# First pair, last pair and end of a hybrid encoder step: banks, order and token halves

## The chip, the cores and the metric

The kernel runs on one core of a Trainium2 chip. The metric is the device time of one execution in microseconds (us). TensorE (PE, with its weight loads PEld), VectorE (DVE), ScalarE (ACT), GpSimd (POOL) and SyncE (SP) run streams of their own and hand work on by semaphores.

## What is computed

One layer for 512 prompt tokens and 32 sample tokens (TOK = 544), with D = 1024, 8 heads of 64, and weights in fp32:

```python
xn = rms_norm(x, g_mix)
u, q, k, v, gates = split(xn @ w_in)                # 512 | 512 | 512 | 512 | 2048 columns
gate_a, gate_b = split(sigmoid(gates + b_gate))
y_pool = (trailing_mean(u) - u) @ w_pool_grp * scale # 4 groups, windows 2, 4, 8, 16
y_sb = stick_breaking(q, k, v)                       # a = exp(log_sigmoid(z) + later log_sigmoid(-z)), causal
x = x + (gate_a * (y_pool @ w_pool_up) + gate_b * (y_sb @ w_sb_up)) @ w_out
x = x + square(relu(rms_norm(x, g_mlp) @ w_up)) @ w_down
x = x + sigmoid(rms_norm(x, g_ple) @ w_ple_gate) * (p @ w_ple_proj)
y = rms_norm(x, g_final)
```

k, v and the pooling state are outputs too.

## The kernel before

Features lie on partitions, tokens on columns. A result of 128 features x 544 tokens takes two PSUM banks of 272 columns, a "slot" (banks 2s and 2s+1). Products in fp32 precision are made of three passes over high and low parts: hi*hi, hi*lo, lo*hi. Each weight tile (512 KB) is loaded by SP into `raw`, its high part is made by ScalarE (`split`, L691, later `hi`, L699), its low part by VectorE (`split`, L1448, later `ahead`, L1456), in a ring of four (`AHEAD` = 3 tiles ahead). SP loads tile t when the low part of tile t-2 is made.

The order of the work is written out by hand in each engine's block. Stage 1 has four pairs of heads, `pair(i)`, each with eight tiles: q, k, v, u, then four gate tiles; pair 0 and pair 3 are written out, 1 and 2 are a loop. TensorE's tile is 48 matmuls. A head's attention goes: `scores` (z into banks 4 to 6), `chain` on ScalarE (Abs, Exp, Ln), `stick` on VectorE (L1532), masks on GpSimd (L634), `stick_later`, `stick_hi` and `stick_lo` (sums over keys, high and low parts), `sums` on TensorE (L1114), `prob` on ScalarE (L778), masks, `prob_hi` and `prob_lo` (L1553), `outputs` on TensorE (L1140). The second head's `sums` and `outputs` run within the next pair. `v_rows` transposes v into bank 7. VectorE multiplies each result by the inverse norm `rn`, which scales tokens, since the norm is taken beside the products: `square` (L715) and `add_square` (L1473) sum the squares, `first_stats` sums over partitions by a matmul with -1 (L1091), `variance` (L1481), `root` (Ln, Exp), `root_step` (L1486 to L1488).

In pair 0 results 0, 1, 2 lie in slots 0, 1, 2 and result 3 (u) in slot 0 again (`result_slot`). TensorE's order there: tiles 0, 1, 2 with the norm's sums (into banks 6 and 7) behind step 1 of tile 2, tile 3, `scores(0)`, `v_rows`, tiles 4 and 5, `sums(0)`, tile 6, `outputs(0)`, `scores(1)`, tile 7.

In pair 3 the four group maps of the pooling (`group`, L1042) need the high and low parts of the means (`mean_hi`, `mean_lo` L1573); those of groups 2 and 3 are made after ScalarE's `chain(1)` and VectorE's `stick(1)`.

The last stage makes the gate of the embedding in two groups of seven products (`product_of`, L1352, SIDES A11, S1, S2, S4, S3, A12, A22; a Strassen-like scheme in which each result is a quarter: half of the group's features x half of the tokens). The second group is followed by four `embedding` tiles (L1042 to L1044), `embedded` (L1881 multiply, L1883 add to x), ScalarE's squares (L1021), five sums over partitions (`stat3`, L1430), Ln and Exp (L1028, L1031), L1481 to L1488, then the final scaling of eight tiles of 128 x 544: six by VectorE (L1916), two by GpSimd (L676), each stored by SP (L570).

## Time and profile before

| | us |
|---|---|
| median of 3 runs | 793.26 (792.95 to 793.46) |
| the profiled execution | 793.77 |
| its span | 791.9 |
| PE busy | 773.7 (98%) |
| DVE busy | 494.8 (62%) |
| ACT busy | 381.5 (48%) |
| POOL busy | 96.9 (12%) |

The span is the time from the first to the last event that the profiler saw on the core. TensorE's busy time is modelled at its end (a matmul is pipelined), so the starts of its matmuls are to be read, and the idle time in brackets behind a row.

### The profile page before, as it was taken

To read this page: it belongs to the slowest core of one execution; us is meant where nothing else is said; L and a number is where in the kernel's file an instruction comes from. 1 tells how busy PE (TensorE), PEld (TensorE's weight loads), DVE (VectorE), ACT (ScalarE), POOL (GpSimd) and SP (SyncE) were. 2 spreads that over 40 slices of the span, in tenths; PEclk is the share of its full clock that TensorE was granted. 3 is DMA by queue.
4 is the path that set the end of the run, shared out by engine and by line. 5 is a ranking of instruction groups with operands and counts; after the bars stand their busy time and mean duration, and the time that the engine had idled before them with its cause. 6 is when DMAs were issued, how large, how long until landed. Compare 5 with 4: busy or idle time off the path is not lost.

```text
span 791.9 us, 14329 instructions
## 1 busy us (share of the span) xinstructions
PE 773.7 (98%) x6050; PEld 765.2 (97%) x6050; DVE 494.8 (62%) x606; ACT 381.5 (48%) x443; POOL 96.9 (12%) x169
## 2 busy tenths in 40 slices
PE   8899999999999999999999999999999999999993
PEld 8899999999999899999999999999999999999993
DVE  5876566566566547787763367434763367677965
ACT  6554534535575443665641255213642155555643
POOL 1040140150150000020001100020001100100001
PEclk9999999999999999999999999999999999999998
DMA  7342231232221316786566847587575856826402
GB/s 236 99 125 74 70 120 53 82 105 56 98 90 55 107 54 206 240 202 178 179 171 168 202 160 206 139 188 183 158 192 145 204 171 180 195 82 161 119 1 113
DMA packets 33097, 110.18 MB, mean 139 GB/s; under 512 B 4496, under 2 KB 4496, under 8 KB 33040
## 3 DMA queue, kind: packets, MB, share of 16 engines
q1 hardware_dynamic: 24768, 84.72, 32.4%
q0 software_dynamic: 6016, 21.04, 14.9%
q10 hardware_dynamic: 2256, 3.60, 1.3%
q8 instruction: 44, 0.72, 0.4%
q14 instruction: 13, 0.11, 0.0%
HBM read 94.33 MB, written 4.52 MB: 125 GB/s over the span
## 4 chain that ended last, share of the span: by engine, by line
PE 90%; DVE 5%; ACT 2%; issue 1%; DMA 1%; SPq 1%; DVEq 0%; ACTq 0%
PE psum L1352 24%; PE psum L1061 19%; PE psum L1067 19%; PE psum L1064 19%; PE psum L1114 1%; DMA xt<-x_t 1%; PE psum L1042 1%; PE psum L1142 1%; PE psum L1043 1%; PE psum L1044 1%; PE psum L1140 1%; PE psum L1430 1%; PE psum L1102 1%; DVE work L1473 1%; PE psum L1101 1%
## 5 line engine op out<-in xcount | busy, mean ns | idle before, releaser
L699 ACT ACTIVATE w_hi<-raw_more 128x1024 fp32r<-128x1024 f32 x84 | 88.7, 1056 | 133.0 <-PE psum L1067 100.7
L1064 PE MATMUL psum<-b_lo,w_hi 128*128 128x272 f32 x688 | 142.0, 288 | 0.0
L1061 PE MATMUL psum<-b_hi,w_hi 128*128 128x272 f32 x672 | 139.3, 288 | 0.0
L1067 PE MATMUL psum<-b_hi,w_lo 128*128 128x272 f32 x672 | 138.8, 288 | 0.0
L1061 PE MATMUL psum<-a_hi,w_hi 128*128 128x272 f32 x576 | 120.8, 291 | 3.3 <-DVE a_lo L1462 1.2
L1456 DVE TENSOR_TENSOR w_lo<-raw_more,w_hi 128x1024 fp32r<-128x1024 f32 x84 | 102.2, 1222 | 34.6 <-ACT w_hi L699 34.3
L1067 PE MATMUL psum<-a_hi,w_lo 128*128 128x272 f32 x576 | 119.0, 288 | 0.0
L1064 PE MATMUL psum<-a_lo,w_hi 128*128 128x272 f32 x576 | 118.8, 288 | 0.0
L1352 PE MATMUL psum<-u_hi,w_hi 128*128 128x272 f32 x560 | 115.9, 288 | 0.2 <-ACT h_of L933 0.2
L1352 PE MATMUL psum<-u_hi,w_lo 128*128 128x272 f32 x560 | 115.7, 288 | 0.0
L1352 PE MATMUL psum<-u_lo,w_hi 128*128 128x272 f32 x560 | 115.5, 287 | 0.0
L1064 PEld LDWEIGHTS psum<-b_lo,w_hi 128*128 128x128 f32 x688 | 108.1, 188 | 0.0
L1061 PEld LDWEIGHTS psum<-b_hi,w_hi 128*128 128x128 f32 x672 | 105.4, 188 | 0.8 <-issue 0.7
L1067 PEld LDWEIGHTS psum<-b_hi,w_lo 128*128 128x128 f32 x672 | 105.1, 189 | 0.0
L1061 PEld LDWEIGHTS psum<-a_hi,w_hi 128*128 128x128 f32 x576 | 90.2, 188 | 4.4 <-DVE a_lo L1462 2.0
L1064 PEld LDWEIGHTS psum<-a_lo,w_hi 128*128 128x128 f32 x576 | 90.5, 189 | 0.0
L1067 PEld LDWEIGHTS psum<-a_hi,w_lo 128*128 128x128 f32 x576 | 90.0, 189 | 0.0
L1352 PEld LDWEIGHTS psum<-u_hi,w_hi 128*128 128x128 f32 x560 | 87.9, 188 | 0.5 <-issue 0.4
L1352 PEld LDWEIGHTS psum<-u_lo,w_hi 128*128 128x128 f32 x560 | 88.3, 188 | 0.0
L1352 PEld LDWEIGHTS psum<-u_hi,w_lo 128*128 128x128 f32 x560 | 87.5, 188 | 0.0
L1742 DVE TENSOR_TENSOR xt<-psum,xt 128x544 f32<-128x544 f32 x40 | 28.9, 723 | 88.2 <-PE psum L1067 88.2
L1448 DVE TENSOR_TENSOR w_lo<-raw,w_hi 128x1024 fp32r<-128x1024 f32 x41 | 51.8, 1265 | 41.5 <-ACT w_hi L691 41.3
(245 smaller groups left out, 1010.3 us busy)
## 6 DMA issues: line engine op xcount, KB each, us to landing
raw_more<-w_tiles SPq DMA_DIRECT2D x84, 512.0 KB, 4.3
raw<-w_tiles SPq DMA_DIRECT2D x66, 512.0 KB, 3.5
raw_more<-w_tiles POOLq DMA_DIRECT2D x16, 512.0 KB, 6.7
raw_more<-raw_more POOLq DMA_DIRECT2D x14, 512.0 KB, 8.3
xt<-x_t SPq DMA_DIRECT2D x8, 272.0 KB, 6.2
y_t<-xt SPq DMA_DIRECT2D x8, 272.0 KB, 2.5
raw<-w_tiles POOLq DMA_DIRECT2D x4, 512.0 KB, 7.6
raw_more<-raw POOLq DMA_DIRECT2D x3, 512.0 KB, 6.4
```

The costliest lines, as they stand in the source:

```text
L699: act.activation(w_hi[:, t % W_RING, :, :].rearrange("p k c -> p (k c)"), src, ACT.Copy)\
L1042: pe.matmul(out, hi, rhi, start=first, stop=False, skip_group_check=True)
L1043: pe.matmul(out, hi, rlo, start=False, stop=False, skip_group_check=True)
L1044: return pe.matmul(out, lo, rhi, start=False, stop=last, skip_group_check=True)
L1061: pe.matmul(base[:, h, :], w_hi[:, s, wk, :], at(hi, k, h * HALF, (h + 1) * HALF), start=(opens and q == 0), stop=False, skip_group_check= ...
L1064: pe.matmul(base[:, h, :], w_hi[:, s, wk, :], at(lo, k, h * HALF, (h + 1) * HALF), start=False, stop=False, skip_group_check=True)
L1067: mm = pe.matmul(base[:, h, :], w_lo[:, s, wk, :], at(hi, k, h * HALF, (h + 1) * HALF), start=False, stop=(closes and q == len(ks) - 1), s ...
L1101: pe.matmul(z, b_lo[:, keys], b_hi[:, both], start=(b != 3), stop=False, skip_group_check=True)
L1352: mm = pe.matmul(out[:, two, :], w_part[:, t % W_RING, 2 * k + two, :], u_part[:, op, k, :], start=(OPENS[s] and k == 0 and w_part is w_hi ...
L1448: dve.tensor_tensor(w_lo[:, s, :, :].rearrange("p k c -> p (k c)"), raw[:, t % RAW_RING, :], w_hi[:, s, :, :].rearrange("p k c -> p (k c)" ...
L1456: dve.tensor_tensor(w_lo[:, t % W_RING, :, :].rearrange("p k c -> p (k c)"), src, w_hi[:, t % W_RING, :, :].rearrange("p k c -> p (k c)"), ...
L1742: dve.tensor_tensor(halves(xt[:, m, :]), slot(n), halves(xt[:, m, :]), ALU.add).then_inc(taken, 1)
```

## The change

- `result_slot`: result 3 (the first u) gets slot 3 (banks 6 and 7).
- The first norm's sums go into the free columns of banks 0 to 3 in four pieces, behind step 3 of tile 2 instead of step 1.
- Pair 0: tiles 3 and 4 come ahead of the first scores, then `v_rows`, tiles 5 and 6, `sums(0)`, tile 7, `outputs(0)`, `scores(1)`. The other engines' orders follow: ScalarE splits tiles 5, 6 and 7 ahead of `chain(0)`, VectorE splits 6 and 7 and reads the first gate ahead of `stick(0)`, and reads v's low half and splits tile 8 ahead of `stick_lo(0)`.
- Pair 3: the means of groups 2 and 3 are split ahead of `chain(1)` and `stick(1)`.
- The last group is followed by halves of tokens: five products, the second token half's two embeddings, A12, the first embedding of the first token half, the second half's norm sum, A22, the last embedding, the first half's sum. Sigmoids, squares, roots, scaling and stores go by quarters and halves; 16 stores of 136 KB stand for 8 of 272 KB. ScalarE loads the sigmoid table and the logarithm table once more.

```diff
@@ -100,10 +100,21 @@
         seq.extend((("down", c, q), q % 4, False) for q in range(KT))
     group("ple", 0, 0, "stat2")
     seq.extend((("proj", q), (2 + q) % 4, False) for q in range(KT // 2))
-    group("ple", 1, 1)
-    seq.extend((("proj", KT // 2 + q), q, False) for q in range(KT // 2))
-    seq.append((("stat3",), 0, False))
+    for what in LAST_ORDER:
+        if what[0] == "ple":
+            seq.append((what, 2 + (not IN_X[what[2]]), BY_ACT[what[2]]))
+        else:
+            seq.append((what, {"pj": what[-1], "stat3": 3 * what[-1]}[what[0]], False))
     return seq
+LAST_ORDER = ([("ple", 1, s) for s in range(5)] + [("pj", 1, 0), ("pj", 1, 1), ("ple", 1, 5), ("pj", 0, 0),
+              ("stat3", 1), ("ple", 1, 6), ("pj", 0, 1), ("stat3", 0)])
+PLE_PLACE = ((0, 1, 2, 3, 4, 5, 6, 7), (0, 1, 2, 3, 4, 6, 7, 5))
...
@@ -175,7 +187,7 @@
 def result_slot(n):
-    return (n if n < 3 else 0) if n < 4 else (n - N_ATT + 2) % 4 if n >= N_ATT else n % 2
+    return n if n < 4 else (n - N_ATT + 2) % 4 if n >= N_ATT else n % 2
...
@@ -385,7 +398,21 @@
             return h[:, half, :, :].rearrange("p n t -> p (n t)")
-        rn_ps = psum[:, 2:4, 0:HALF]
+        first_sums = psum[:, 0:4, HALF:HALF + HALF // 2]
...
@@ -558,17 +588,16 @@
...
-            sp.wait_ge(out_done, 16 * KT)
+            for nth, i in enumerate((1, 0)):
+                for k in range(KT):
+                    if k % 4 == 3:
+                        m = POOL_LAST[k // 4]
+                        sp.wait_ge(fin_pool, len(POOL_LAST) * nth + k // 4 + 1)
+                    else:
+                        m = BY_DVE[k - k // 4]
+                        sp.wait_ge(fin_done, len(BY_DVE) * nth + k - k // 4 + 1)
+                    sp.dma_start(y_t[m, :, tokens(i)], xt[:, m, tokens(i)]).then_inc(out_done, 16)
+            sp.wait_ge(out_done, 16 * 2 * KT)
...
@@ -669,11 +698,13 @@
...
+            for nth, i in enumerate((1, 0)):
+                pool.wait_ge(rn_done, nth + 1)
+                pool.wait_ge(fin_done, len(BY_DVE) * nth + 1)
+                for m in POOL_LAST:
+                    x = xt[:, m, tokens(i)]
+                    pool.tensor_tensor(x, x, rn[:, tokens(i)], ALU.mult).then_inc(fin_pool, 1)
...
@@ -814,18 +849,32 @@
...
                 act.dma_start(k_t[i, :, :], ev[:, 1, 0:TOK]).then_inc(kv_out[0], 16)
-                if not first:
-                    prob(1, i - 1)
+                if first:
+                    split(AHEAD + 2)
+                    act.wait_ge(taken, 3)
+                    act.dma_start(v_t[i, :, :], ev[:, 2, 0:TOK]).then_inc(kv_out[1], 16)
+                    split(AHEAD + 3)
+                    split(AHEAD + 4)
+                    chain(0, i)
+                    values_hi(i)
+                    split(AHEAD + 5)
+                    stick_hi(0, i)
+                    split(AHEAD + 6)
+                    prob(0, i)
+                    split(AHEAD + 7)
+                    prob_hi(0, i)
+                    chain(1, i)
...
@@ -842,10 +891,11 @@
                 if last:
                     group_hi(0)
                     group_hi(1)
-                chain(1, i)
-                if last:
+                    act.wait_ge(z_done, HEADS)
                     mean_hi(2)
                     mean_hi(3)
+                chain(1, i)
                 split(AHEAD + 7, i, S1_PER, 7)
                 if last:
...
+                act.wait_ge(res_done, KT // 2 + LAST_QUARTERS.index((half, i)) + 1)
+                act.activation(made(UP_GROUPS + 1, half, i), last_x(half, i), ACT.Square).then_inc(sq_done, 1)
+            def half_root(nth, i):
+                n = NTH[("stat3", i)]
+                r = ev[:, 1, tokens(i)]
+                act.wait_ge(full, n + 1)
+                act.activation(r, slot(n)[:, 0, :], ACT.Ln, scale=-1.0 / D_MODEL, bias=eps[:, 0:1]).then_inc(log_done, 1)
+                act.wait_ge(log_done, nth)
+                act.activation(r, r, ACT.Exp, scale=-0.5).then_inc(root_done, 1)
...
+            quarter_sigmoid(0, 1)
...
+            quarter_sigmoid(1, 1)
+            quarter_square(0, 1)
+            quarter_square(1, 1)
+            quarter_sigmoid(0, 0)
+            tables(LOG_EXP)
+            half_root(4, 1)
+            quarter_square(0, 0)
+            tables(SIGMOID)
+            quarter_sigmoid(1, 0)
+            tables(LOG_EXP)
+            quarter_square(1, 0)
+            half_root(5, 0)
+            act.wait_ge(rn_done, 2)
+            act.activation(rn_ps, rn[:, tokens(0)], ACT.Copy).then_inc(rn_copied, 1)
...
@@ -1176,10 +1245,13 @@
             def first_stats(q):
-                if q == 1:
+                if q == 3:
                     pe.wait_ge(const_made, N_CONST)
                     pe.wait_ge(sq_added, KT)
-                    stats(None).then_inc(stat0, 1)
+                    for b in range(4):
+                        mm = pe.matmul(first_sums[:, b, :], negone[:, :].bitcast(F32),
+                                       acc[:, b * HALF // 2:(b + 1) * HALF // 2], start=True, stop=True)
+                    mm.then_inc(stat0, 1)
...
@@ -1193,20 +1265,25 @@
                     weights(2)
                     dense(result(2), 2, ALL, A, aside=first_stats).then_inc(full, 1)
                     tile(3, i)
-                else:
-                    tile(0, i)
-                    tile(1, i)
-                    sums(1, i - 1)
-                    tile(2, i)
-                if first:
-                    pe.wait_ge(var_done, 1)
-                    pe.wait_ge(taken, 3)
-                else:
-                    outputs(1, i - 1)
+                    tile(4, i)
+                    pe.wait_ge(taken, 4)
+                    scores(0, i)
+                    v_rows(i)
+                    tile(5, i)
+                    tile(6, i)
+                    sums(0, i)
+                    tile(7, i)
+                    outputs(0, i)
+                    scores(1, i)
+                    return
+                tile(0, i)
+                tile(1, i)
...
+            def last_embedding(i, half):
+                t, n = t_ple(1, T_UP), NTH[("pj", i, half)]
+                weights(t)
+                place_for(n)
+                for k in range(PLE // P):
+                    c = slice(k * TOK + i * HALF, k * TOK + (i + 1) * HALF)
+                    for w_part, b_part in ((w_hi, b_hi), (w_hi, b_lo), (w_lo, b_hi)):
+                        for two in range(2):
+                            wk = k * (KT // 2) + 2 * half + two
+                            mm = pe.matmul(slot(n)[:, two, :], w_part[:, t % W_RING, wk, :], b_part[:, c],
+                                           start=(k == 0 and w_part is w_hi and b_part is b_hi),
+                                           stop=(k == PLE // P - 1 and w_part is w_lo), skip_group_check=True)
...
+            def last_sums(i):
+                n = NTH[("stat3", i)]
+                place_for(n)
+                pe.wait_ge(sq_added, 3 * KT + KT // 2 + i)
+                squares = [(acc[:, tokens(i)], 0)]
+                for half in range(2 - 2 * i):
+                    q = made(UP_GROUPS + 1, half, i)
+                    squares += [(q[:, two, :], KT // 2 + LAST_QUARTERS.index((half, i)) + 1) for two in range(2)]
+                for k, (of, nth) in enumerate(squares):
+                    if nth:
+                        pe.wait_ge(sq_done, 3 * KT + nth)
+                    mm = pe.matmul(slot(n)[:, 0, :], negone[:, :].bitcast(F32), of, start=(k == 0),
+                                   stop=(k == len(squares) - 1), skip_group_check=True)
+                mm.then_inc(full, 1)
...
+            for what in LAST_ORDER:
+                if what[0] == "ple":
+                    product_of(t_ple(1, what[2]), NTH[what], what[2]).then_inc(full, 1)
+                elif what[0] == "pj":
+                    last_embedding(what[1], what[2])
...
+                    last_sums(what[1])
...
@@ -1628,21 +1739,29 @@
...
-                                  rn[:, SEQ:TOK], ALU.mult).then_inc(taken, 1)
+                pool_input(i)
                 if first:
+                    split(AHEAD + 3)
+                    split(AHEAD + 4)
+                    gate(0, i)
                     stick(0, i)
-                    split(AHEAD + 3)
                     stick_later(0, i)
+                    values_lo(i)
+                    split(AHEAD + 5)
+                    stick_lo(0, i)
+                    gate(1, i)
+                    split(AHEAD + 6)
+                    gate(2, i)
+                    split(AHEAD + 7)
+                    prob_lo(0, i)
+                    gate(3, i)
+                    head_out(0, i)
+                    stick(1, i)
+                    stick_later(1, i)
+                    stick_lo(1, i)
...
@@ -1661,13 +1780,13 @@
                 head_out(0, i)
                 if last:
                     group_lo(1)
+                    mean_lo(2)
+                    mean_lo(3)
                 else:
                     split(AHEAD + 7, i, S1_PER)
                 stick(1, i)
                 if last:
-                    mean_lo(2)
                     gate(3, i)
...
+            def scaled_quarter(side):
+                n, i = NTH[("ple", 1, SIDES.index(side))], 1 if side == "S4" else 0
+                c = made(UP_GROUPS + 1, 0, i)
+                dve.wait_ge(taken, taken_count(n))
+                dve.tensor_tensor(c, c, rn_of[i], ALU.mult).then_inc(rel_done, 1)
+            def gated_quarter(half, i):
+                nth, n = LAST_QUARTERS.index((half, i)), NTH[("pj", i, half)]
+                h = made(UP_GROUPS + 1, half, i)
+                dve.wait_ge(psig_done, 2 + nth + 1)
+                dve.wait_ge(full, n + 1)
+                dve.tensor_tensor(h, slot(n), h, ALU.mult).then_inc(taken, 1)
+                dve.wait_ge(taken, taken_count(n))
+                dve.tensor_tensor(last_x(half, i), last_x(half, i), h, ALU.add).then_inc(res_done, 1)
...
+            def half_rms(nth, i):
...
+                dve.wait_ge(root_done, nth)
+                link(dve.scalar_tensor_tensor(out=t, in0=r, scalar=-0.5, in1=r, op0=ALU.mult, op1=ALU.mult))
+                dve.wait_ge(taken, taken_count(n))
+                link(dve.tensor_tensor(t, t, var[:, tokens(i)], ALU.mult))
+                dve.scalar_tensor_tensor(out=rn[:, tokens(i)], in0=t, scalar=1.5, in1=r, op0=ALU.add, op1=ALU.mult)\
+                   .then_inc(rn_done, 1)
...
+                ahead(T_PLE + T_UP + 1 + s)
+                if s < KT // 2:
+                    add_square(s, 3 * KT)
+                if SIDES[s] in ("S4", "S3"):
+                    add_quarter(UP_GROUPS + 1, NTH[("ple", 1, s)], s)
+                if SIDES[s] == "S4":
+                    scaled_quarter("S4")
+                if SIDES[s] == "S3":
+                    scaled_second(UP_GROUPS + 1, "S3")
+            gated_quarter(0, 1)
+            gated_quarter(1, 1)
+            dve.wait_ge(sq_done, 3 * KT + KT // 2 + 2)
+            two, other = made(UP_GROUPS + 1, 0, 1), made(UP_GROUPS + 1, 1, 1)
+            link(dve.tensor_tensor(two, two, other, ALU.add))
+            link(dve.tensor_tensor(acc[:, tokens(1)], acc[:, tokens(1)], two[:, 0, :], ALU.add))
+            dve.tensor_tensor(acc[:, tokens(1)], acc[:, tokens(1)], two[:, 1, :], ALU.add).then_inc(sq_added, 1)
+            add_quarter(UP_GROUPS + 1, NTH[("ple", 1, 5)], 5)
+            scaled_quarter("A12")
+            gated_quarter(0, 0)
+            half_rms(4, 1)
+            scaled_second(UP_GROUPS + 1, "A22")
+            dve.wait_ge(rn_done, 1)
+            for m in BY_DVE[:2]:
+                finished(m, 1, rn[:, tokens(1)])
+            gated_quarter(1, 0)
+            dve.wait_ge(res_done, KT // 2 + 4)
+            for m in BY_DVE[2:]:
+                finished(m, 1, rn[:, tokens(1)])
+            half_rms(5, 0)
+            dve.wait_ge(rn_done, 2)
+            for m in BY_DVE:
+                if m == BY_DVE[0]:
+                    finished(m, 0, rn[:, tokens(0)])
+                else:
+                    dve.wait_ge(rn_copied, 1)
+                    finished(m, 0, rn_ps)
```

## Rows read from the trace of the kernel before

**Rows 1.** Waits of TensorE over the span: waiter, releaser, us in total, times, longest.
```profile
PE psum L1061 <- DVE ev L1591: 1.2, 1, 1.2
PE psum L1042 <- DVE b_lo L1574: 0.6, 2, 0.3
```
**Rows 2.** Timeline, TensorE, pair 0: start us, us, engine, line, operation, [idle before <-releaser].
```profile
23.16 1.16 PE L1091 MATMUL psum<-work,negone 128*128 128x272 f32 x4 [0.35 <-DVE work L1473]
...
36.06 0.39 PE L1101 MATMUL psum<-b_hi,b_lo 128*128 128x512 f32 x1
...
37.27 0.62 PE L1152 MATMUL psum<-ident,ev 128*128 128x128 f32 x4
38.70 0.49 PE L1061 MATMUL psum<-a_hi,w_hi 128*128 128x272 f32 x2 [0.80 <-DVE upad L1636]
```
**Rows 3.** Timeline, VectorE, pair 0.
```profile
24.69 0.72 DVE L1481 TENSOR_SCALAR work<-psum 128x544 f32<-128x544 f32 x1
...
33.71 1.23 DVE L1448 TENSOR_TENSOR w_lo<-raw,w_hi 128x1024 fp32r<-128x1024 f32 x1
...
36.48 1.23 DVE L1448 TENSOR_TENSOR w_lo<-raw,w_hi 128x1024 fp32r<-128x1024 f32 x1
...
41.35 1.49 DVE L1532 SCALAR_TENSOR_TENSOR work<-psum,work 128x1280 f32<-128x1280 f32 x1 [2.80 <-ACT work L765]
...
48.83 0.55 DVE L1549 TENSOR_TENSOR later_lo<-later,later_hi 128x384 fp32r<-128x384 f32 x1
```
**Rows 4.** The page's DMA issues: count, KB each, us to landing.
```profile
raw<-w_tiles SPq DMA_DIRECT2D x66, 512.0 KB, 3.5
```
**Rows 5.** Timeline, GpSimd: the masks behind the stick steps of the first two heads.
```profile
42.91 1.96 POOL L634 TENSOR_SCALAR_AFFINE_SELECT work<-work 128x128 f32<-128x128 f32 x4 [38.85 <-DVE work L1532]
...
69.44 1.03 POOL L634 TENSOR_SCALAR_AFFINE_SELECT work<-work 128x128 f32<-128x128 f32 x4 [9.48 <-DVE work L1532]
```
**Rows 6.** Timelines around the start of pair 1, VectorE, ScalarE, TensorE.
```profile
67.88 1.48 DVE L1532 SCALAR_TENSOR_TENSOR work<-psum,work 128x1280 f32<-128x1280 f32 x1
...
80.00 0.72 DVE L1497 TENSOR_TENSOR ev<-psum,rn 128x544 f32<-128x544 f32 x1 [0.20 <-PE psum L1067]
...
86.04 1.49 DVE L1553 TENSOR_TENSOR b_lo<-work,b_hi 128x1280 fp32r<-128x1280 f32 x1
...
82.36 1.24 ACT L778 ACTIVATE work<-psum 128x1280 f32<-128x1280 f32 x1 [0.31 <-PE psum L1114]
...
79.80 0.40 PE L1114 MATMUL psum<-b_hi,negtri 128*128 128x512 f32 x1
...
88.22 0.40 PE L1140 MATMUL psum<-b_hi 128*128 128x512 f32 x1
```
**Rows 7.** Timeline, TensorE: the start of pool part 0 behind the group maps.
```profile
247.71 0.49 PE L1061 MATMUL psum<-mean_hi,w_hi 128*128 128x272 f32 x2 [0.34 <-issue]
```
**Rows 8.** The chain of waits (start us, us, what) and TensorE's timeline, last group.
```profile
748.28 21.01 PE psum L1352 x168
...
776.10 3.83 PE L1430 MATMUL psum<-h_two,negone 128*128 128x272 f32 x16
```
**Rows 9.** Timelines, ScalarE and VectorE: a table load, a 544-wide and a 272-wide step.
```profile
771.23 1.28 ACT L725 ACT_TABLE_LOAD   x1
...
782.92 0.72 DVE L1488 SCALAR_TENSOR_TENSOR rn<-ev 128x544 f32<-128x544 f32 x1
...
37.70 0.43 DVE L1633 TENSOR_TENSOR upad<-psum,rn 128x272 f32<-128x272 f32 x1
```
**Rows 10.** The view of the tile y_t: issue durations in ns, first and last start; landing.
```profile
L570 SPq DMA_DIRECT2D y_t<-xt x8: 332/400/652, 784.5 to 788.3; - x8
...
DMA to landing us min/median/max: 2.1/2.5/3.1
```
**Rows 11.** Stretches of the end: busy us of each engine, granted clock, DMA share, GB/s.
```profile
785.00:785.50 0.50, 0.00 (x0) 0.00 (x0) 0.50 (x2) 0.00 (x0) 0.50 (x1) 0.58 0.29 113
...
790.00:791.00 1.00, 0.00 (x0) 0.00 (x0) 0.00 (x0) 0.00 (x0) 0.00 (x0) 0.50 0.95 370
```

More of the change, by code:

```diff
@@ L134, in staged_loads @@
     seq.append(("proj", 0))
-    seq.extend((UP_GROUPS + 1, what) for what in LOADS)
+    seq.extend((UP_GROUPS + 1, what) for what in LOADS[:5])
     seq.append(("proj", 1))
+    seq.extend((UP_GROUPS + 1, what) for what in LOADS[5:])
     return seq
@@ L385, in made_half, with tokens, last_x @@
             return h[:, half, :, :].rearrange("p n t -> p (n t)")
-        rn_ps = psum[:, 2:4, 0:HALF]
+        first_sums = psum[:, 0:4, HALF:HALF + HALF // 2]
+        rn_ps = psum[:, 2, 0:HALF]
+        def tokens(i):
+            return slice(i * HALF, (i + 1) * HALF)
+        def last_x(half, i):
+            return xt[:, 4 * half + 2:4 * half + 4, tokens(i)]
+        LAST_QUARTERS = ((0, 1), (1, 1), (0, 0), (1, 0))
+        BY_DVE = [m for m in range(KT) if m not in POOL_LAST]
         rn_twice = rn[:, :].unsqueeze(1).broadcast_to([P, 2, TOK])
@@ L1017, in _ @@
-            tables(LOG_EXP)
-            for q in range(KT // 2, KT):
-                m = PROJ_ORDER[q]
-                act.wait_ge(res_done, q + 1)
-                act.activation(h_two[:, m // 4, m % 2, :], xt[:, m, :], ACT.Square).then_inc(sq_done, 1)
+            for s in range(T_UP):
+                n = NTH[("ple", 0, s)]
+                ahead(t_ple(0, s))
+                if s == 0:
+                    act.wait_ge(ulo_done, 3 * KT)
+                if s == 3:
+                    act.wait_ge(taken, taken_count(NTH[("stat2",)]))
+                    root(3)
+                    embedding_hi(0)
+                    embedding_hi(1)
+                if s == 5:
+                    tables(SIGMOID)
+                if s == T_UP - 1:
+                    gate_sigmoid(0, 0)
+                if BY_ACT[s]:
+                    copy_quarter(UP_GROUPS, n, s)
@@ L1085, in tile @@
                 dense(pair_result(j, i), j % W_RING, ALL, A).then_inc(full, 1)
-            def stats(n):
-                out = psum[:, 6:8, 0:HALF] if n is None else result(n)
-                for h in range(2):
-                    mm = pe.matmul(out[:, h, :], negone[:, :].bitcast(F32), acc[:, h * HALF:(h + 1) * HALF],
-                                   start=True, stop=True)
-                return mm
             def scores(hh, i):
@@ L1432, in _ @@
-            mm.then_inc(full, 1)
+            def last_embedding(i, half):
[11 more added lines that the diff above has]
+                mm.then_inc(full, 1)
@@ L1434, in _ @@
+            group_of("ple", 0, t_ple(0, 0), 3 * KT // 2, "stat2", 3 * KT)
+            for q in range(KT // 2):
+                embedding(q)
+            for what in LAST_ORDER:
[3 more added lines that the diff above has]
+                    last_embedding(what[1], what[2])
+                else:
+                    last_sums(what[1])
         @block.vector
@@ L1908, in _ @@
[L1908 to L1918 removed]
+            for s in range(T_UP):
+                ahead(t_ple(0, s))
+                if s == 3:
+                    statistics("stat2")
+                if SIDES[s] in ("S4", "S3", "A12"):
+                    add_quarter(UP_GROUPS, NTH[("ple", 0, s)], s)
+                if s == 3:
+                    root_step(3)
+                if SIDES[s] == "S3":
+                    scaled_second(UP_GROUPS, "S3")
+                    embedding_lo(0)
+                    embedding_lo(1)
+                if SIDES[s] == "A12":
+                    scaled_first(UP_GROUPS)
@@ new lines, in _ @@
+            scaled_second(UP_GROUPS, "A22")
+            ahead(t_ple(0, T_UP))
+            for q in range(KT // 2):
+                embedded(q)
+            def scaled_quarter(side):
[5 more added lines that the diff above has]
+                nth, n = LAST_QUARTERS.index((half, i)), NTH[("pj", i, half)]
+                h = made(UP_GROUPS + 1, half, i)
+                dve.wait_ge(psig_done, 2 + nth + 1)
[3 more added lines that the diff above has]
+                dve.tensor_tensor(last_x(half, i), last_x(half, i), h, ALU.add).then_inc(res_done, 1)
@@ new lines, in finished @@
+            def finished(m, i, factor):
+                x = xt[:, m, tokens(i)]
+                dve.scalar_tensor_tensor(out=x, in0=x, scalar=g_fin[:, m:m + 1], in1=factor, op0=ALU.mult,
+                                         op1=ALU.mult).then_inc(fin_done, 1)
+            for s in range(5):
+                ahead(T_PLE + T_UP + 1 + s)
+                if s < KT // 2:
+                    add_square(s, 3 * KT)
[3 more added lines that the diff above has]
+                    scaled_quarter("S4")
+                if SIDES[s] == "S3":
+                    scaled_second(UP_GROUPS + 1, "S3")
```

177 lines of the change are left out of this document (59 added, 118 removed).

## The prediction

> **What bounds the kernel now.** I read the waits of TensorE over the whole span first, then its timeline through the first head, then VectorE's and ScalarE's beside it, the chain through the last group, and the rows of the output stores. The matmul engine has no gap of note between 39 and 776 us; its waits with a partner elsewhere are short ones in the first 39 us and around 245 us [rows 1]. A product of the last group takes 3.00 us (168 matmuls in 21.01 for the seven), so one matmul of 272 columns starts every 0.125 us and a tile of 48 takes 6.0 us, 6.04 with its start [rows 8]. So time can be won only by closing those gaps, and after the last product, where 16 us hold the last norm, the scaling and the stores. A change of order is then worth what it closes less what it opens.
>
> **First pair, what goes.** Before, the sum for the first norm starts at 23.16 behind VectorE's adds; tile 3 waits 1.2 us for the read of q; tile 4 waits for the read of u until 38.70 although the transposes, four of 0.11, end at 37.7 [rows 1, 2]. Three gaps, 0.5 + 1.3 + 1.0. After, the sums come behind step 3 of tile 2: 21.14 + 4 x 0.752 = 24.15, no wait (23.16 less 0.5 of gap less two steps of 0.752 is 21.15). They are the same columns in four pieces, about 0.95 us, and end, with 0.2 for the drain, at 25.3. Tile 3, in banks of its own, runs from 28.25 to 34.3.
>
> **First pair, what comes.** VectorE read the sums at 24.69, now at 25.33, and from there on it and ScalarE hand over step by step to the low half of tile 4's weights: 33.71 becomes 34.35, done 35.58 [rows 3]. In the old order tile 4 wanted these at 38.70; now it wants them at 34.3 and starts at 35.73. That is a new gap of 1.4 us which no line of the diff mentions. Tile 4 ends at 41.77, scores 1.21 (36.06 to 37.27), transposes 0.45 [rows 2], tiles 5 and 6, and the sums over the stick are wanted at 55.5. Their operands: scores start to VectorE's first stick step is 5.29 (36.06 to 41.35), so 47.06; from there to the last low part 8.03 (41.35 to 48.83 + 0.55) [rows 2, 3]. In the new order nothing of VectorE lies beside the masks, which then take 1.03 rather than 1.96 [rows 5], but the low half of v (0.61) and a weight split (1.15) stand ahead of the low part: 8.03 - 0.93 + 1.76 = 8.86, ready at 55.9, with the signal 56.0. Gap 0.45. ScalarE's splits of tiles 6 and 7 now stand ahead of its chain; tile 7's load is issued when tile 5's low half is done (36.48 + 1.23 + 0.64 = 38.35), a load takes 3.5 [rows 3, 4], the split 1.05, so it ends near 43.0 against scores ready at 43.2: hidden, by 0.2 us only. The rest of the pair (probabilities, outputs) keeps about 0.5 us of room. Against the old kernel, tile 4 and all before it, scores and transposes stand at 35.73 + 1.65 = 37.4 where 38.70 was: 1.3 won, 0.45 given back. **Pair 0: -0.85 us.**
>
> **The second pair pays for the gate tile.** Tile 7 used to run between the second head's scores and the next pair. Now the scores come behind it, so TensorE has 12.1 us, not 18.1, until it wants those sums, and ScalarE and VectorE start the second head's chain 6 us later against it, but had waited 2 us: the stick step stood at 67.88, 0.14 behind the start of tile 8 (79.80 less two tiles is 67.74) [rows 6]; now it comes 4.1 behind (5.29 less the 1.21 of the scores). Lateness 3.95. The sums themselves still come in time: their low part is ready at 4.1 + 8.03 - 0.93 = +11.2 at the latest, by the first head's rows, and wanted at +12.1. What is queued behind them is not: VectorE runs without a pause from that step to the k of pair 1, where it had 0.20 us of room (80.00), so k is 3.75 late; ScalarE's next probability waits behind the copies of k, with 0.31 of room (82.36), so it is 3.45 late; the low part of the probabilities, 86.04 to 87.53, is in a row with it, and the outputs of the second head took it at 88.22 [rows 6], 0.6 of room. **New gap at the outputs of pair 1: 2.85 us.** It is taken once: the wait itself puts TensorE behind the other two again, and pairs 2 and 3 keep the old order.
>
> **Last means ahead of the chain.** The third and fourth group maps wait for VectorE's low means, 0.6 us in all [rows 1], and pool part 0 starts at 247.71 [rows 7]. After, the gate tile ends at 244.6 and map 2 at 245.35; ScalarE's copy (0.7) is done at 246.3, VectorE's low half (0.8) at 247.06, pool part 0 at 247.15. The chain of the last head starts 1.3 later (two copies of means), its low part is ready at 252.2 and wanted at 253.2: hidden, with 1.0 of room. **-0.55 us.**
>
> **The end.** Products start at 748.28 and take 3.00 each; four small ones of 1.5 follow; the norm's sums end at 779.93; rn is done at 783.64; the stores are issued from 784.5 to 788.3 [rows 8 to 10]. Their bytes flow from about 785.3 to 790.95 [rows 11]: 8 x 272 KB in 5.6 us, 398 GB/s. The stores are bound by bandwidth. After, by order: five products to 763.3, two half embeddings to 766.3, A12 to 769.3, one to 770.8. VectorE is the engine in demand: its 544-wide steps cost 0.76 each in a row (0.72 for one), its 272-wide about 0.45 (0.43 for one) [rows 9]. From the S3 result at 763.4: add, scale, two gated quarters (767.9), ScalarE's square, three adds (770.25), A12 added 770.9. The sum of the second token half waits for that add to give its bank: 0.3 us. A22 then ends at 774.6 and the last half embedding at 776.1. VectorE meanwhile: first token quarter to 773.9, the root of the second token half to 775.95, A22 scaled to 776.6, two final rows, gated quarter 777.3 to 778.8; ScalarE's square to 779.5; two fp32 sums of 0.45 (16 passes of 0.23 in 3.83 [rows 8]); the sums end at 780.7, 0.8 later than before. Two more table loads of 1.28 [rows 9] lie on ScalarE while VectorE has other work: one ends at 776.5, just ahead of A22 at 776.6. Then all steps are half as wide: the logarithm and four VectorE steps take 2.3 for 3.7: rn at 783.05, first store at 783.55. Half the bytes have gone by then. Eight stores at a median of 0.40 put the last at 786.4; it lands in the shortest landing of before, 2.1 [rows 10], or less, since it is half as large: 788.4, and the span closes 0.5 behind, near 788.9 where it was 791.9. **-3.0 us** (from -1.8, if a store costs 0.5 and the sigmoid waits for its table, to -3.5).
>
> **Sum.** -0.85 + 2.85 - 0.55 - 3.0 = -1.55 us. The profiled run took 793.77 (span 791.9 and 1.9 around it); it gives 792.2. The median of the runs is 0.5 lower, so 791.7, and I say 791.8. What this kernel can be told from no change by is about 0.2%, 1.6 us; the forecast lies on that line.
>
> **Rivals.**
> (a) No gap in pair 1: if the lateness were absorbed, 791.8 - 2.85 = 788.9. Against it: VectorE's rows from 67.88 to 80.00 follow each other, with 0.20 of idle at the end [rows 6]. Chance 0.10.
> (b) VectorE and GpSimd get in each other's way in the first head. Masks took 1.96 us beside a VectorE subtraction from SBUF and 1.03 without [rows 5]; if they take the long time again, the first sums wait 1.4, not 0.45: 792.75. Chance 0.13. The Trainium skill, GPSIMD Engine Reference, section Specifications, says that GpSimd shares its SBUF interfaces with VectorE, with contention when VectorE has two SBUF inputs. By that rule, the masks here have no such partner and take the short time; the trace agrees.
> (c) The end gives 1.8 only: 793.0. Chance 0.07.
> (d) Slower: the gap of 2.85 us in pair 1 lets TensorE's clock fall to 1.2 GHz. The scores and the tile behind it would take twice their time, some 6 us: 797.8. It decides if the granted clock falls within 2.9 us of idleness. At the end the last matmul is over at 779.9 and the grant is full until about 785.05 (0.58 over 785.0 to 785.5) [rows 11], 5 us later: against it. Chance 0.04. The Trainium skill, TensorE: Matmul & The Clock Gate, section What's actually happening, says the gate falls back to half rate after idleness; by it a gap of this kind is a risk, and the row shows one of nearly twice its length at full clock.
> (e) Slower: the lateness is not used up by one wait and comes back where pair 2 begins. Price another 2.85: 794.7. It would if the two engines were still over 0.6 us late against TensorE when pair 1 has its outputs. Against it: the wait ends as the low part does, which is 0.7 us nearer than in the old rows (87.53 to 88.22) [rows 6], and the next chain starts only when TensorE has the next scores. Chance 0.04.
> The forecast: 0.62, itself 790.6 to 793.0, since the unknown gaps of the first pair are 0 to 1.4 and those of the end 1 us.
>
> **Chances.** Faster by over 0.2% (under 791.7): (a) and a little under half of the forecast, 0.38. Slower by over 0.2%: (d), (e) and the edge of the rest, 0.09. Within: 0.53. The range, 789.6 to 793.7, leaves out (a), (d) and (e).
>
> **What would show it.** A wait for a weight's low half ahead of tile 4 at 34.3 of 1.4 us; one of 0 to 1.4 at the first sums; none at tile 3; one of 2.5 to 3.1 at the second head's outputs in pair 1, near 87, behind VectorE's low part, and none like it in pairs 2 and 3; pool part 0 0.5 us behind the gap's start; last norm's sums read 0.5 to 1.2 later than now against the last group's start; eight stores behind rn at 0.4 each. If the wait in pair 1 is missing, the working of the second pair is wrong and the kernel is clearly faster; if the stores take 5 us in spite of half the bytes, that of the end is.

## The result and the profile after

The changed kernel takes 794.73 us (median of 18 runs, 793.4 to 795.56) against 793.23 (18 runs, 792.87 to 794.25): a ratio of 1.0016, interval 1.001 to 1.0023. It is slightly slower, by 1.3 to 1.5 us, and lies 1.0 us above the range of the forecast, which had it 1.5 us faster.

| us | before | after |
|---|---|---|
| profiled span | 791.9 | 792.5 |
| mean granted clock | 0.996 | 0.992 |
| last group's first product | 748.28 | 750.54 |
| from there to the end of the span | 43.6 | 41.96 |

First, as in [rows 1], the waits of TensorE over the whole span (waiter, releaser, us in total, times, longest):

```profile
PE psum L1209 <- DVE b_lo L1650: 2.6, 1, 2.6
PE psum L1519 <- ACT h_two L1074: 2.6, 1, 2.6
...
PE psum L1138 <- DVE w_lo L1548: 1.3, 1, 1.3
...
PE psum L1119 <- DVE gates L1664: 0.6, 1, 0.6
PE psum L1183 <- DVE later_lo L1646: 0.3, 1, 0.3
```

The old waits for `ev` and `upad` are gone. In their place stand five others. The prediction named three of them as waits (`b_lo`, `w_lo`, `later_lo`); the other two, for `h_two` and `gates`, lie where its times leave TensorE idle at the end and ahead of pool part 0. TensorE's timeline says where (start us, us, line, operation, [idle before <-releaser]); the rows answer [rows 2, 7] and the last of [rows 6]:

```profile
23.23 1.09 PE L1252 MATMUL psum<-work,negone 128*128 128x136 f32 x8
...
34.66 0.52 PE L1138 MATMUL psum<-a_hi,w_hi 128*128 128x272 f32 x2 [1.33 <-DVE w_lo L1548]
...
54.96 0.51 PE L1183 MATMUL psum<-b_hi,negtri 128*128 128x512 f32 x1 [0.32 <-DVE later_lo L1646]
...
89.25 0.49 PE L1209 MATMUL psum<-b_hi 128*128 128x512 f32 x1 [2.62 <-DVE b_lo L1650]
...
248.78 0.39 PE L1119 MATMUL psum<-b_hi 128*128 128x272 f32 x1 [0.56 <-DVE gates L1664]
...
249.89 0.49 PE L1138 MATMUL psum<-mean_hi,w_hi 128*128 128x272 f32 x2
```

These starts are to be read with one correction: in this execution the inputs came earlier (`x_t` landed in 5.2 us in the median, 6.2 in the profile before), and the first sums, predicted at 24.15, stand at 23.23. All that follows is 0.92 us early, which is not of the change.

In pair 1 VectorE and ScalarE stand so; the rows answer [rows 6]:

```profile
81.89 0.72 DVE L1593 TENSOR_TENSOR ev<-psum,rn 128x544 f32<-128x544 f32 x1
...
83.96 1.24 ACT L809 ACTIVATE work<-psum 128x1280 f32<-128x1280 f32 x1
...
87.63 1.49 DVE L1650 TENSOR_TENSOR b_lo<-work,b_hi 128x1280 fp32r<-128x1280 f32 x1
```

Against the old rows, each 1.77 earlier as tile 8 is, k is 3.7 us late (3.75 predicted) and the probability 3.4 (3.45 predicted).

And this the prediction had thought unlikely: the stretches behind that wait (length and busy us of PE, PEld, DVE, ACT, POOL, then granted clock, DMA share, GB/s).

```profile
89.00:90.00 1.00, 0.75 (x4) 0.66 (x4) 0.84 (x3) 0.00 (x0) 0.00 (x0) 1.00 0.68 250
90.00:91.00 1.00, 1.00 (x7) 1.00 (x7) 0.10 (x1) 0.00 (x0) 0.00 (x0) 0.75 0.56 225
91.00:92.00 1.00, 1.00 (x4) 0.81 (x4) 0.95 (x2) 0.00 (x0) 0.00 (x0) 0.50 0.00 0
92.00:93.00 1.00, 1.00 (x6) 1.00 (x5) 0.43 (x1) 0.00 (x0) 0.00 (x0) 0.50 0.00 0
93.00:94.00 1.00, 1.00 (x6) 1.00 (x7) 0.00 (x0) 0.76 (x1) 0.00 (x0) 0.54 0.00 0
```

The last column but two falls to 0.50, the 1.2 GHz level, and TensorE is busy all through it: 0.25 + 0.50 + 0.50 + 0.46 = 1.7 us of full speed are lost there. In the kernel before no stretch ahead of 785 us is under full grant.

The sum of this profile closes. Head start -0.92, pair 0 -0.85 (tile 8 starts at about 65.97 where 67.74 was), the wait of pair 1 +2.8 (86.45 to 89.25), the clock +1.7, the last means -0.53 make +2.2; the last group starts 2.26 later. The end gives -1.65 where -3.0 was predicted.

### The profile page after: what moved, and what is told of

Read it like the earlier page. It is cut to its first block, busy times and chain, and to the rows that moved or that the text cites. A ratio compares the mean times of both kernels' runs of the same rounds, so it can differ in the third digit from the quotient of the medians.

```text
span 792.5 us, 14360 instructions
## 1 busy us (share of the span) xinstructions
PE 773.3 (98%) x6046; PEld 764.7 (96%) x6046; DVE 498.1 (63%) x620; ACT 384.8 (49%) x449; POOL 96.0 (12%) x171
## 4 chain that ended last, share of the span: by engine, by line
PE 82%; issue 7%; DVE 6%; ACT 3%; POOL 1%; DVEq 0%; ACTq 0%; POOLq 0%
PE psum L1429 22%; PE psum L1138 18%; PE psum L1144 17%; PE psum L1141 17%; PE psum L1183 1%; PE psum L1211 1%; PE psum L1171 1%; PE psum L1209 1%; PE psum L1170 1%; ACT w_hi L730 1%; PE psum L1190 0%; PE psum L1195 0%; DVE w_lo L1548 0%; PE psum L1119 0%; POOL work L663 0%
## 5 line engine op out<-in xcount | busy, mean ns | idle before, releaser
L1138 PEld LDWEIGHTS psum<-a_hi,w_hi 128*128 128x128 f32 x576 | 90.5, 189 | 3.3 <-DVE a_lo L1562 1.8
```

Source lines behind the costliest of these rows:

```text
L1138: pe.matmul(base[:, h, :], w_hi[:, s, wk, :], at(hi, k, h * HALF, (h + 1) * HALF), start=(opens and q == 0), stop=False, skip_group_check= ...
```

## The experiments

Each ratio is to the kernel before on the same chip (medians 793.09, 792.93 and 793.14 in the three groups e1 to e4, e5, e6). Pairs 1 and 2, a loop in the changed kernel, are written out on an engine wherever only pair 1 is changed there.

| run | median us | ratio, interval |
|---|---|---|
| e1_old_first_pair | 790.8 | 0.9972 (0.9962 to 0.9983) |
| e2_old_end | 795.89 | 1.0032 (1.0020 to 1.0043) |
| e3_pair1_reordered | 790.0 | 0.9962 (0.9948 to 0.9976) |
| e4_clock_kept | 792.9 | 1.0001 (0.9992 to 1.0010) |
| e5_control | 789.91 | 0.9961 (0.9947 to 0.9974) |
| e5_two_queues | 789.79 | 0.9960 (0.9947 to 0.9974) |
| e5_gpsimd_later | 789.40 | 0.9956 (0.9942 to 0.9970) |
| e5_both | 789.31 | 0.9954 (0.9941 to 0.9968) |
| e6_half_wait | 791.63 | 0.9982 (0.9973 to 0.9991) |
| e6_both_control | 789.38 | 0.9955 (0.9942 to 0.9969) |
| e6_waits_first | 789.55 | 0.9955 (0.9942 to 0.9969) |
| e6_end_busy | 789.51 | 0.9954 (0.9941 to 0.9968) |

### Which part costs

**e1_old_first_pair**: means and end as changed, the first pair with its banks and order as before.

```diff
-    return n if n < 4 else (n - N_ATT + 2) % 4 if n >= N_ATT else n % 2
+    return (n if n < 3 else 0) if n < 4 else (n - N_ATT + 2) % 4 if n >= N_ATT else n % 2
...
-                if q == 3:
+                if q == 1:
```

> The changed kernel with the order, the banks and the first norm's sums of pair 0 as before; the last means and the end stay changed. My theory: the loss lies where the first pair's new order hands over to the second (a wait of 2.8 us and 1.4 us at half clock), and the end and the last means win 1.65 and 0.55. So 2.2 us faster than the kernel before, ratio 0.9972 (0.996 to 0.998), no TensorE wait at the outputs of pair 1. Rival: the end itself loses by its slower stores; then this kernel is at 1.000 or above.

Measured 0.9972: means and end together give 2.2 us. TensorE has no wait at the outputs of pair 1 in its trace, and full grant until 778.5.

**e2_old_end**: first pair and means as changed, the last group whole as before.

```diff
-    for what in LAST_ORDER:
+    group("ple", 1, 1)
+    seq.extend((("proj", KT // 2 + q), q, False) for q in range(KT // 2))
+    seq.append((("stat3",), 0, False))
```

> The changed kernel with the end of the kernel before (one product order, 8 stores); first pair and last means stay changed. My theory: -0.85 in pair 0, +2.8 wait, +1.4 half clock, -0.55 at the means: 2.8 us slower than before, ratio 1.0035 (1.0025 to 1.0045). Rival, that the end costs: not over 1.001.

Measured 1.0032, so the first pair costs some 3 us where the prediction had it at +2.0. The stretches of its pair 1 show why this varies from one execution to the next; here the wait ends at 89.60:

```profile
88.00:89.00 1.00, 0.00 (x0) 0.00 (x0) 1.00 (x1) 0.00 (x0) 0.00 (x0) 0.98 0.00 0
89.00:90.00 1.00, 0.40 (x1) 0.41 (x2) 1.00 (x2) 0.00 (x0) 0.00 (x0) 0.50 0.79 197
...
94.00:95.00 1.00, 1.00 (x7) 1.00 (x6) 0.00 (x0) 0.41 (x1) 0.00 (x0) 0.50 0.00 0
95.00:96.00 1.00, 1.00 (x7) 1.00 (x7) 0.00 (x0) 0.97 (x2) 0.00 (x0) 0.60 0.00 0
```

The same wait of 2.6 us, but the clock falls inside it, at 89.0, and is back only at 95.8. From 89.6 on TensorE works 6.2 us at half grant. What that costs is read from its starts, outputs to the next sums over the stick:

```profile
89.60 0.79 PE L1152 MATMUL psum<-b_hi 128*128 128x512 f32 x1 [2.62 <-DVE b_lo L1570]
...
113.52 0.40 PE L1126 MATMUL psum<-b_hi,negtri 128*128 128x512 f32 x1
```

These are 23.9 us; in e4 below, with full grant all through, the same work takes 21.1 (89.04 to 110.16), and in the changed kernel 22.7. So 2.8 us are lost here and 1.6 there.

### The wait or the clock

**e3_pair1_reordered** takes the wait away. In pair 1 ScalarE takes the second head's probabilities ahead of the copies of k, and VectorE makes their low part right behind `kst`.

```diff
+                early = isinstance(i, int) and i == 1
+                if early:
+                    prob(1, 0)
+                    prob_hi(1, 0)
                 act.wait_ge(taken, 2 + i * S1_PER)
...
                 dve.tensor_copy(kst[:, i, :], k[:, SEQ:TOK])
+                if early:
+                    prob_lo(1, 0)
```

> The changed kernel; in pair 1 alone ScalarE makes the second head's probabilities and their high part ahead of its copies of k, and VectorE their low part ahead of k's low halves (pairs 1 and 2 written out instead of looped on these two engines). My theory: the low part is then ready at 19.9 us behind the start of the pair's first tile against 20.5 wanted, the wait of 2.8 goes, the clock stays full, and the kernel is 0.85 + 0.55 + 1.65 = 3.0 us faster than before, ratio 0.9962 (0.9950 to 0.9975). Rival: the lateness only moves to the scores of pair 1's first head, which need k: then the ratio stays at 1.000 or above.

**e4_clock_kept** leaves the wait and takes away the idleness: eleven throwaway matmuls into a bank that nobody reads at that time. The output is the same.

```diff
+                if isinstance(i, int) and i == 1:
+                    pe.wait_ge(y_done, 1)
+                    for _ in range(11):
+                        pe.matmul(psum[:, 7, 0:P], negone[:, :].bitcast(F32), negone[:, :].bitcast(F32),
+                                  start=True, stop=True)
```

> The changed kernel with 11 throwaway matmuls (128 columns, fp32, into the idle bank 7) ahead of the second head's outputs in pair 1, so that TensorE is busy for some 2.4 of the 2.8 us of its wait (pairs 1 and 2 written out on TensorE). My theory: the wait stays, the granted clock does not fall, the scores behind it take 1.2 instead of 2.4 us: 1.4 us faster than the changed kernel, ratio to before 1.000 (0.999 to 1.001). Rival: the slow matmuls have another cause, or the time is lost by the wait alone: as the changed kernel, 1.0016 or more.

Timeline of e4 at the outputs, and one stretch behind them:

```profile
86.32 2.62 PE L1287 MATMUL psum<-negone 128*128 128x128 f32 x22
89.04 0.50 PE L1209 MATMUL psum<-b_hi 128*128 128x512 f32 x1
```

```profile
91.00:92.00 1.00, 1.00 (x10) 1.00 (x9) 0.96 (x2) 0.16 (x1) 0.00 (x0) 1.00 0.00 0
```

The outputs start as late as before, with the clock at 1.00, and the kernel is at 1.0001: 1.2 us better than the changed one by the ratios, 1.8 by the medians, where 1.7 were read off the stretches. (The changed kernel did not run again beside it, so the price is known to be between these two.) So the fall of the clock is a cost of its own. e3 has neither: the outputs run through in this timeline, with no idle time before them.

```profile
86.61 0.40 PE L1215 MATMUL psum<-b_hi 128*128 128x512 f32 x1
```

0.9962 is 4.3 to 4.7 us better than the changed kernel, and the wait (2.8) and the clock (1.7) are 4.5. That e3 is also 0.8 us better than e1 is the gain of pair 0, predicted at 0.85. No run has the loop written out and nothing else, but the traces show that this alone gains nothing: from the sums over the stick of pair 1's first head to pool part 0 it is 137.95 us in the changed kernel with its loop, and 137.96 and 137.95 in e3 and e4.

**e6_half_wait** shortens the wait instead: only `prob(1, 0)` moves on ScalarE, the rounding and VectorE's order stay.

```diff
+                if early:
+                    prob(1, 0)
                 act.wait_ge(taken, 2 + i * S1_PER)
```

> The changed kernel with one step of ACT moved in pair 1: the second head's exponentials of pair 0 are taken before the two copies of k, and their rounding stays where it is (pairs 1 and 2 are written out on ACT for that). The low half that the outputs wait for should then be made at 86.3 instead of 87.6, so that TensorE waits about 1.4 us there instead of 2.6. Theory (the clock falls behind a long wait and not behind one of half the length): it stays at full speed at 89 to 94, and the run gains 1.35 us of wait and the 1.45 us of half speed: 1.0016 minus 0.0035, 0.9981 of the kernel before. Rival (any wait of over a microsecond makes it fall there): only the 1.35 us are gained, 0.9999, and the windows at 89 to 94 show 0.5.

Its timeline, and the stretches around:

```profile
88.69 0.49 PE L1213 MATMUL psum<-b_hi 128*128 128x512 f32 x1 [1.21 <-DVE b_lo L1654]
```

```profile
88.00:89.00 1.00, 0.31 (x1) 0.30 (x2) 1.00 (x2) 0.00 (x0) 0.00 (x0) 1.00 0.57 123
89.00:90.00 1.00, 1.00 (x8) 0.93 (x7) 0.37 (x2) 0.00 (x0) 0.00 (x0) 1.00 0.94 381
90.00:91.00 1.00, 1.00 (x9) 0.92 (x8) 0.67 (x1) 0.00 (x0) 0.00 (x0) 1.00 0.05 20
```

0.9982, where the theory had 0.9981. In these profiles the wait of 1.2 us keeps the clock and those of 2.6 us in pair 1 lose it; taking 1.4 us off the wait brought 2.7 to 3.1.

### The end

The kernel of e3 is the base here. Its changes to pair 1 are kept.

> The kernel of e3_pair1_reordered once more, as the base of the three that run beside it: 0.9962 of the kernel before again. Its last half of the rows is stored by eight issues on SP at 0.48 us each, the first at 782.2, the last at 785.6, and the bytes flow at 280 GB/s with a DMA share of 0.80 until 787.0.

It repeats, 0.9961.

**e5_two_queues** deals the last half's eight stores out to SP and ACT.

```diff
+                    if nth == 1 and k % 2:
+                        continue
...
+            for k in range(1, KT, 2):
...
+                act.dma_start(y_t[m, :, tokens(0)], xt[:, m, tokens(0)]).then_inc(out_act, 16)
+            act.wait_ge(out_act, 16 * KT // 2)
```

> The kernel of e5_control with the last half's eight stores dealt out to two queues: the even ones stay on SP, the odd ones are issued by ACT, which has nothing else left. Theory (the end is bound by SP's issues, 0.48 us for each store, since the landing stays at 1.7 to 2.1 us for all sixteen and no backlog builds up): the last store is issued when its tile is ready (784.3) instead of at 785.6, the flow rises well over 280 GB/s, and the span is 1.2 us shorter: 0.9947. Rival (the rows of 1088 bytes bound the transfers at 280 GB/s): the flow stays at 280 GB/s, the landing of the last stores lengthens, and the span is unchanged: 0.9962.

The view of `y_t` in the control (issue durations ns, first and last start, time to landing) and a stretch:

```profile
L599 SPq DMA_DIRECT2D y_t<-xt x16: 332/448/456, 775.3 to 785.9; - x16
...
DMA to landing us min/median/max: 1.7/1.9/1.9
```

```profile
785.00:786.00 1.00, 0.00 (x0) 0.00 (x0) 0.00 (x0) 0.00 (x0) 0.00 (x0) 0.50 0.82 283
```

The same with two queues:

```profile
L602 SPq DMA_DIRECT2D y_t<-xt x12: 332/413/457, 774.7 to 785.0; - x12
L1127 ACTq DMA_DIRECT2D y_t<-xt x4: 338/368/468, 783.4 to 785.0; - x4
...
DMA to landing us min/median/max: 1.7/1.9/2.6
```

```profile
785.00:786.00 1.00, 0.00 (x0) 0.00 (x0) 0.00 (x0) 0.00 (x0) 0.00 (x0) 0.50 1.05 360
```

Half of the theory is shown: the 280 GB/s were the pace of one queue's issues (0.48 us for 136 KB), since with two the same rows of 1088 bytes flow at 360. The gain did not come. Counted from the first finished tile of the last half (782.02 and 782.39), the bytes are through 0.7 us earlier, but the span ends after 6.4 us in both. The last landing grew to 2.6 us, and from it to the end lie 1.1 us where the control has 0.6.

**e5_gpsimd_later** takes GpSimd's share of the first half from beside VectorE's last addition of the embedding.

```diff
-                pool.wait_ge(fin_done, len(BY_DVE) * nth + 1)
+                pool.wait_ge(fin_done, len(BY_DVE) * nth + (1 if nth else 3))
```

> The kernel of e5_control with one number changed: for the first half GpSimd starts its two tiles when three of VectorE's are finished, not one, so that it no longer runs beside the addition of the last embedding. Theory (the two engines slow each other when both read two operands from SBUF): that addition takes 0.72 us again instead of 1.25, everything behind it comes 0.5 us earlier, and the collision moves to the finished rows of the first half, where VectorE has 0.7 us of slack: 0.9956. Rival (the 1.25 us has another cause, or the rows of the first half now hold up the square root): 0.9962.

In the changed kernel and in this one, VectorE's and GpSimd's timelines:

```profile
780.45 1.25 DVE L2038 TENSOR_TENSOR xt<-xt,h_two 128x544 f32<-128x544 f32 x1
...
779.54 1.57 POOL L707 TENSOR_TENSOR xt<-xt,rn 128x272 f32<-128x272 f32 x2 [41.56 <-DVE xt L2056]
```

```profile
776.17 0.72 DVE L2047 TENSOR_TENSOR xt<-xt,h_two 128x544 f32<-128x544 f32 x1
776.93 2.75 DVE L2065 SCALAR_TENSOR_TENSOR xt<-xt,vec,rn 128x272 f32<-128x272 f32 x4
```

The addition is back at 0.72, the collision has moved to four steps that take 2.75 instead of 1.74 and have that room, and the kernel is 0.5 us faster in the median than the control beside it. The intervals overlap, and so do the runs by 0.1 (789.28 to 789.75 against 789.64 to 790.13), so the 0.5 rests on the timelines and on e5_both, which is e5_two_queues with this same edit: 789.31 against 789.79, and there the runs do not overlap (789.25 to 789.48 against 789.63 to 790.51).

**e5_both** has both of these edits.

> Both changes of e5_two_queues and e5_gpsimd_later. Theory: they add up, 1.2 and 0.5 us: 0.9941. If both rivals hold: 0.9962.

0.9954: what GpSimd's edit gives, and nothing from the second queue. **e6_both_control** repeats it, **e6_waits_first** moves ACT's old waits ahead of its stores (three of them, the text on record says five):

```diff
+            act.wait_ge(pool_out, 32)
+            for s in kv_out:
+                act.wait_ge(s, 16 * PAIRS)
             for k in range(1, KT, 2):
...
-            act.wait_ge(pool_out, 32)
-            for s in kv_out:
-                act.wait_ge(s, 16 * PAIRS)
```

> The kernel of e5_both once more, as the base of the next two: 0.9954 of the kernel before.

> The kernel of e5_both, where the flow of the last stores had risen to 360 GB/s and their bytes were through 0.7 us earlier, while the span ended no earlier. One change: ACT's five waits for transfers that landed long ago stand before its last stores, and not behind the wait for them. Theory (those waits ran one after the other at the end of the program and took what the second queue gave): 0.5 us shorter, 0.9948. Rival (the second queue's own last landing is late by as much): 0.9954.

0.9955 both. Those waits were not what took the gain; the cause stays open.

**e6_end_busy** fills TensorE's wait in the last sums, 2.6 us in the changed kernel and 2.1 in its own base, e6_waits_first.

```diff
+                if i == 0:
+                    for _ in range(8):
+                        pe.matmul(slot(n)[:, 0, 0:P], negone[:, :].bitcast(F32), negone[:, :].bitcast(F32),
+                                  start=True, stop=True, skip_group_check=True)
```

> The kernel of e6_waits_first, with eight throwaway 128x128 matmuls in TensorE's 2.6 us wait ahead of the last four matmuls of the last sums; they write the bank that the sums then overwrite, so the output is the same. Theory (in some executions the clock falls before these four matmuls, which then take 2.2 us instead of 1.2, as in the profile of e5_two_queues): up to 1.0 us shorter where that happened, 0.3 us in the median, 0.9944. Rival (it falls behind them in nearly all executions, and nothing waits for TensorE any more): 0.9948.

No gain in the median, 789.51 against 789.55. The loss that it guards against is real in some executions: the profile of e1 has the last four matmuls at half speed,

```profile
778.97 2.18 PE L1501 MATMUL psum<-h_two,negone 128*128 128x272 f32 x4 [2.58 <-ACT h_two L1056]
```

and VectorE then waits 1.71 us for ScalarE's root where it waits 0.80 in the changed kernel. e6_end_busy has them at full speed, with its eight throwaways as 16 passes ahead:

```profile
774.05 1.95 PE L1532 MATMUL psum<-negone 128*128 128x128 f32 x16
...
777.63 1.18 PE L1541 MATMUL psum<-h_two,negone 128*128 128x272 f32 x4 [0.26 <-ACT h_two L1083]
```

Its five runs lie within 0.12 us (789.44 to 789.56), those of e6_waits_first within 1.0, but e6_waits_first's own profile has these matmuls at full speed too: there the wait of 2.1 us did not lose the clock in time to matter. In the profile of e5_gpsimd_later, with as long a wait, the clock fell at 778.3, between them:

```profile
777.64 1.56 PE L1525 MATMUL psum<-h_two,negone 128*128 128x272 f32 x4 [2.05 <-ACT h_two L1080]
```

And of the seven profiles with a wait of 2.6 us at this place two have these matmuls at half speed (e1 and e5_two_queues, 2.18 us) and five at full speed (1.18 to 1.28). So the length of the wait alone does not say whether the clock is lost in time to matter.

## Why the prediction was wrong, point by point

**Pair 0: right.** The first sums came with no wait; tile 4 waits 1.33 for its weights (1.4 predicted), the first sums over the stick 0.32 (0.45), tile 3 not at all. Worth 0.85 by the start of tile 8, 0.8 by e3 against e1.

**The wait of pair 1: right.** 2.8 us from the end of the tile to the outputs, 2.85 predicted, in the row predicted (`b_lo` of the probabilities), once, and none in pairs 2 and 3. Rivals (a) and (e) fall with it. Rival (b) falls too: no wait at the first sums but the 0.32.

**Rival (d) had the missing mechanism, and was dismissed at 0.04.** Of its 6 us 1.7 came, and it needs the shortfall of the end beside it to reach the time measured (see the sum below). The step that failed is the evidence against it: "the last matmul is over at 779.9 and the grant is full until about 785.05". That was one execution of one idle stretch, and I took the 5 us for a limit. A wait of 2.6 us lost the clock in the profiles of the changed kernel and of e2, 1.25 us after TensorE had resumed in the one and 0.6 us before in the other. Its price was wrong as well, 1.7 us (2.8 in e2) and not 6 (by its own rows, 1.21 for the scores and 6.04 for the tile, it would even have been 7.2): the fall lasted 3.4 and 6.8 us and not through scores and a whole tile at half speed. The Trainium skill, TensorE: Matmul & The Clock Gate, section What's actually happening, which the prediction weighed less than its one row, calls the fall a matter of recent idleness and says that its observation doesn't restart with the kernel, so that the point of the change moves from run to run. The two profiles agree.

**The last means: right.** Pool part 0 stands at 249.89, 0.53 nearer than it would be; 0.55 predicted.

**The end: the mechanism right, the size not.** 1.65 instead of 3.0, under the edge that rival (c) had set at 1.8. Two terms were mis-sized. The first is rn: predicted 34.8 us behind the group's first product, measured 35.6 (786.13 less 750.54). 0.53 of the 0.8 is the addition at 1.25 us beside GpSimd, the rest lies in several small steps. The prediction had applied that very effect to the masks, rightly, and not looked for it among the operations that the change sets side by side at the end. The Trainium skill, GPSIMD Engine Reference, section Specifications, names this case (VectorE with two inputs in SBUF), and the trace agrees: 1.25 against 0.72. The second is the stores: the changed kernel's view of `y_t` and a stretch of its end,

```profile
L599 SPq DMA_DIRECT2D y_t<-xt x16: 332/450/707, 779.4 to 790.0; - x16
...
DMA to landing us min/median/max: 1.7/1.9/2.1
```

```profile
789.00:790.00 1.00, 0.00 (x0) 0.00 (x0) 0.00 (x0) 0.00 (x0) 0.00 (x0) 0.50 0.81 279
```

From rn to the end of the span lie 6.4 us where 5.85 were predicted. An issue took 0.45 in the median and one followed the other at 0.48, not at 0.40 (the median of [rows 10], which is how long an issue lasts and not how often one comes); the prediction had a store of 0.5 only as the edge of its range for the end. Half the bytes in as many issues moved the limit from the bytes to the queue: 136 KB each 0.48 us are 290 GB/s, and 279 to 283 flow. The two misses, 0.8 and 0.5, are the 1.3 us that the end fell short.

**The sum.** Predicted -1.55. With the clock (+1.7) and the shortfall (+1.35) it is +1.5, and the medians differ by 1.5. Either of the two alone would have left the time inside the range that ends at 793.7 (793.5 and 793.15); together they took it out.

## What to carry to other kernels

A new wait on TensorE has two prices, its length and the clock behind it: here 2.6 us cost 1.7 to 2.8 us more in pair 1, and 1.2 us cost nothing more; in the last sums waits of 2.6 us cost some 0.9 us in two profiles and nothing in five. One long idle stretch at full clock in a profile is no proof that the next one keeps it; give such a rival a real share, and size it by several stretches. When two engines are set beside each other, and when a transfer is cut in halves, ask again what limits each piece. What ran best here was the change with the second head's probabilities drawn ahead in pair 1 and GpSimd's tiles started later, with or without the second queue: 789.3 to 789.4 us, a ratio of 0.9954 to 0.9956.

## What was not expected of the hardware

- The clock's fall is not tied to the end of the idle time: in one kernel it came 1.25 us after work had resumed (90.5), with TensorE fully busy since 89.25. The time of the changed kernel spreads, its 18 runs going from 793.4 us at a mean clock of 0.994 to 795.5 at 0.990, while the five runs of e5_control, without the wait, lie within 0.5 us. That this one wait makes the spread is not shown: e1, without it, spreads over 1.45 us in eight runs, and e4, with it filled, over 1.9 in eleven.
- A second queue raised the flow of 136 KB stores from 280 to 360 GB/s and lengthened their landing from 1.9 to 2.6 us, so that the end of the program gained nothing.
- A VectorE addition of 128 x 544 with both operands in SBUF took 1.25 us beside a GpSimd product and 0.72 alone, while GpSimd's own two steps took 1.57 instead of 1.48.
